# One-hot operands of the gate matmuls laid out contiguously in a three-layer mixer and expert kernel

## The reference, cut to what matters

```python
def peer(x, w_q, sub_keys, u_tab, v_tab):         # per token: 8 heads, 2 halves of 128 keys
    q = (xt @ w_q).reshape(T, PEER_HEADS, 2, PEER_HALF)
    s = jnp.einsum('thpd,hpkd->thpk', q, sub_keys)
    s_top, i_top = lax.top_k(s, PEER_TOPK)        # 16 best keys i1 and i2 of each half
    cand = s_top[:, :, 0, :, None] + s_top[:, :, 1, None, :]
    best, pos = lax.top_k(cand, PEER_TOPK)        # 16 pairs; expert = i1 * 128 + i2
    gate = jax.nn.softmax(best, axis=-1)
    act = gelu(einsum('td,thkd->thk', xt, u_tab[eid]))
    return einsum('thk,thkd->td', gate * act, v_tab[eid])
```

## Time and profile before

| | us |
|---|---|
| median of 3 runs | 3374.04 (3371.47 to 3375.68) |
| profiled execution, its time | 3377.82 |
| its span | 3376.0 |
| PE busy, PEld busy | 3158.0 (94%), 2855.7 (85%) |
| DVE busy | 2183.4 (65%) |
| ACT busy, POOL busy | 1602.8 (47%), 964.2 (29%) |

### The profile page before, as it was taken

The page is one execution under the profiler, slowest core; times in us unless marked ns, Lnnn a source line. Parts: engine busy times, 40 slices in busy tenths (PEclk is TensorE's granted clock), DMA queues, the critical chain, the costliest instruction groups (busy, mean ns, idle before and its releaser), DMA issues.

```text
span 3376.0 us, 65940 instructions
## 1 busy us (share of the span) xinstructions
PE 3158.0 (94%) x22842; PEld 2855.7 (85%) x22842; DVE 2183.4 (65%) x4301; ACT 1602.8 (47%) x2564; POOL 964.2 (29%) x377
## 2 busy tenths in 40 slices
PE   7899999999998879999999999778789999999998
PEld 6799999888787669999988878677689999988886
DVE  4387477777555345937777755686629667777755
ACT  3355433566455225543356645443345543366654
POOL 5578400000006437960000000256368920000000
PEclk9899999999999779999999999799899999999999
DMA  5445444444664224554444466333254544444554
GB/s 189 133 154 174 162 144 147 144 149 149 214 193 139 86 75 169 173 171 146 144 144 149 148 203 193 102 105 122 68 170 149 179 157 143 144 149 148 162 193 150
DMA packets 141398, 509.40 MB, mean 151 GB/s; under 512 B 16736, under 2 KB 17888, under 8 KB 140912
## 3 DMA queue, kind: packets, MB, share of 16 engines
q1 hardware_dynamic: 141296, 508.04, 45.9%
HBM read 506.93 MB, written 1.05 MB: 150 GB/s over the span
## 4 chain that ended last, share of the span: by engine, by line
PE 80%; DVE 8%; POOL 4%; issue 3%; ACT 2%; DMA 1%; SPq 0%; ACTq 0%; POOLq 0%; DVEq 0%
PE col L504 12%; PE col L506 12%; PE col L505 12%; PE acc L504 11%; PE acc L506 11%; PE acc L505 11%; POOL w_lo L461 4%; PE acc L631 4%; PE col L631 4%; ACT w_hi L719 1%; DVE work L1995 1%; PE acc L1498 1%; PE acc L600 1%; DMA ring<-in_ab_in 0%; DMA ring<-in_v 0%
## 5 line engine op out<-in xcount | busy, mean ns | idle before, releaser
L461 POOL TENSOR_TENSOR w_lo<-ring,w_hi 128x1024 fp32r<-128x1024 f32 x373 | 964.0, 2597 | 1765.7 <-ACT w_hi L719 1763.3
L719 ACT ACTIVATE w_hi<-ring 128x1024 fp32r<-128x1024 f32 x940 | 992.8, 1056 | 667.0 <-PE acc L506 529.5
L504 PE MATMUL col<-x_hi,w_hi 128*128 128x256 f32 (+1 forms) x3904 | 1125.0, 288 | 39.7 <-POOL w_lo L461 31.8
L505 PE MATMUL col<-x_lo,w_hi 128*128 128x256 f32 (+1 forms) x3904 | 1104.3, 283 | 0.0
L506 PE MATMUL col<-x_hi,w_lo 128*128 128x256 f32 (+1 forms) x3904 | 1103.9, 283 | 0.0
L461 DVE TENSOR_TENSOR w_lo<-ring,w_hi 128x1024 fp32r<-128x1024 f32 x567 | 692.6, 1222 | 229.4 <-ACT w_hi L719 229.3
L504 PEld LDWEIGHTS col<-x_hi,w_hi 128*128 128x128 f32 x3904 | 746.9, 191 | 48.6 <-issue 20.0
L506 PEld LDWEIGHTS col<-x_hi,w_lo 128*128 128x128 f32 x3904 | 744.3, 191 | 0.0
L505 PEld LDWEIGHTS col<-x_lo,w_hi 128*128 128x128 f32 x3904 | 741.6, 190 | 0.0
L504 PE MATMUL acc<-w_hi,c_hi 128*128 128x512 f32 x1664 | 670.0, 403 | 15.4 <-DVE c_lo L993 7.9
L506 PE MATMUL acc<-w_hi,c_lo 128*128 128x512 f32 x1664 | 651.6, 392 | 0.0
(11 more groups left out here) (289 smaller groups left out, 2516.7 us busy)
## 6 DMA issues: line engine op xcount, KB each, us to landing
ring<-in_u SPq DMA_DIRECT2D x384, 512.0 KB, 3.2
ring<-in_v SPq DMA_DIRECT2D x384, 512.0 KB, 3.6
ring<-in_wq SPq DMA_DIRECT2D x48, 512.0 KB, 3.2
ring<-in_s_in SPq DMA_DIRECT2D x32, 512.0 KB, 3.5
ring<-in_c_in SPq DMA_DIRECT2D x16, 512.0 KB, 3.2
ring<-in_c_wide SPq DMA_DIRECT2D x16, 512.0 KB, 3.2
ring<-in_s_out SPq DMA_DIRECT2D x16, 512.0 KB, 3.5
ring<-in_s_wide SPq DMA_DIRECT2D x12, 512.0 KB, 3.6
```

Of the source, the lines that this page charges most:

```text
L461: eng.tensor_tensor(k.w_lo[s.slot][:, :], k.ring[s.slot][:, :], k.w_hi[s.slot][:, :].bitcast(F32), ALU.subtract).then_inc(k.lo[s.slot], 1)
L504: pe.matmul(out, a[0], b[0], start=start, stop=False, **kw)
L505: pe.matmul(out, a[0], b[1], start=False, stop=False, **kw)
L719: act.activation(k.w_hi[s.slot][:, :], k.ring[s.slot][:, :], ACT.Copy).then_inc(k.hi[s.slot], 1)
```

## The change

The one-hots are stored with the key number i innermost, so that a token's 128 weights columns and its 64 moving columns are each one contiguous run. DVE still writes them with bf16 operands whose innermost step is one: i1, i2 and the gate parts are each stored twice in a row (`pairs`, `gate_all`), and the compare and multiply run over rows of two elements, with the number table `iota_b` read in pairs and repeated over the tokens. The four-fold table `iota_t` goes. The mask has one buffer instead of two, and `onehots` waits for the previous batch's `oh2` before it writes the mask. The buffers of the one-hots get shapes of their own, the gate's remainder is kept in `oh2`'s room, and the third mixer's scratch (`am`, `e`, `ones`) is mapped to the new buffers. ACT's late one-hots keep their operations and write contiguously.

```diff
-        self.oh1 = room[:, 0:GB * P].bitcast(BF16).rearrange("p (j i t) -> p j i t", j=2, t=GB)
+        self.oh1_all = sb("onehot_i1", [P, 2, GB, P], BF16)
+        self.oh1 = self.oh1_all[:, :, :, :]
+        self.pairs = sb("pairs_of_i1_i2", [P, 2, T, 2], BF16)
+        self.i1, self.i2 = self.pairs[:, 0, :, :], self.pairs[:, 1, :, :]
+        self.oh2_all = sb("gated_onehot_i2", [P, 2, PARTS, GB, EARLY], BF16)
+        self.mask2 = sb("mask_i2", [P, GB, EARLY], BF16)
+        self.gate_all = sb("pairs_of_gate", [P, BATCHES, PARTS, GB, 2], BF16)
+        self.rest = self.oh2.rearrange("p j n t i -> p (j n t i)")[:, 0:2 * T].bitcast(F32)
-        self.iota_t = sb("iota_by_token", [P, P, GB], BF16)
...
-                    ins = pe.matmul(banks[b.slot][:, t * EARLY:(t + 1) * EARLY], k.oh1[:, b.base % 2, :, t],
-                                    k.oh2[:, b.base % 2, n, :, t], start=n == 0, stop=n == PARTS - 1)
+                    ins = pe.matmul(banks[b.slot][:, t * EARLY:(t + 1) * EARLY], k.oh1[:, b.base % 2, t, :],
+                                    k.oh2[:, b.base % 2, n, t, :], start=n == 0, stop=n == PARTS - 1)
...
-                act.activation(k.oh1[:, 1, :, t], k.iota_b[:, :], ACT.Abs, bias=k.neg_i1[:, at])\
+                act.activation(k.oh1[:, 1, t, :], k.iota_b[:, :], ACT.Abs, bias=k.neg_i1[:, at])\
...
-        own.do(dve.tensor_scalar(k.i1[:, :], k.neg_i1[:, :], -1.0, None, ALU.mult))
-        own.do(dve.tensor_copy(k.i2[:, :], k.acc[0][:, T:2 * T]))
+        own.do(dve.tensor_scalar(k.i1, k.neg_i1[:, :].unsqueeze(2).to_broadcast([P, T, 2]), -1.0, None, ALU.mult))
+        own.do(dve.tensor_copy(k.i2, k.acc[0][:, T:2 * T].unsqueeze(2).to_broadcast([P, T, 2])))
...
-            own.do(dve.tensor_copy(k.gate[:, n, :], rest))
+            own.do(dve.tensor_copy(k.gate[:, :, n, :, :], rest.unsqueeze(3).to_broadcast([P, BATCHES, GB, 2])))
...
-            dve.tensor_tensor(k.mask2[:, slot, :, :], k.iota_t[:, at:at + EARLY, :],
-                              k.i2[:, tokens].unsqueeze(1).to_broadcast([P, EARLY, GB]), ALU.is_equal)\
+            if wait:
+                dve.wait_ge(k.oh_ready, b.index() + g0)
+            dve.tensor_tensor(mask, pairs[:, at // 2:(at + EARLY) // 2, :].unsqueeze(1).to_broadcast(shape),
+                              k.i2[:, tokens, :].unsqueeze(2).to_broadcast(shape), ALU.is_equal)\
                .then_inc(k.mask_ready, 1)
             if slot == 0 or not late:
-                dve.tensor_tensor(k.oh1[:, slot, :, :], k.iota_t[:, :, :],
-                                  k.i1[:, tokens].unsqueeze(1).to_broadcast([P, P, GB]), ALU.is_equal)
+                shape = [P, GB, P // 2, 2]
+                dve.tensor_tensor(k.oh1[:, slot, :, :].rearrange("p t (i two) -> p t i two", two=2),
+                                  pairs.unsqueeze(1).to_broadcast(shape),
+                                  k.i1[:, tokens, :].unsqueeze(2).to_broadcast(shape), ALU.is_equal)
             dve.wait_ge(k.mask_ready, b.index() + (g0 + 1))
-            shape = [P, PARTS, EARLY, GB]
-            dve.tensor_tensor(k.oh2[:, slot, :, :, :], k.mask2[:, slot, :, :].unsqueeze(1).to_broadcast(shape),
-                              k.gate[:, :, tokens].unsqueeze(2).to_broadcast(shape), ALU.mult)\
+            shape = [P, PARTS, GB, EARLY // 2, 2]
+            dve.tensor_tensor(k.oh2[:, slot, :, :, :].rearrange("p n t (i two) -> p n t i two", two=2),
+                              mask.unsqueeze(1).to_broadcast(shape),
+                              k.gate[:, bass.ds(b.index(), 1), :, :, :].rearrange("p b n t two -> p (b n) t two")
+                              .unsqueeze(3).to_broadcast(shape), ALU.mult)\
                .then_inc(k.oh_ready, 1)
```

More of the change, by code:

```diff
@@ L1072, in peer @@
         w.next(k.i1_ready)
-        own.do(dve.tensor_scalar(k.i1[:, :], k.neg_i1[:, :], -1.0, None, ALU.mult))
-        own.do(dve.tensor_copy(k.i2[:, :], k.acc[0][:, T:2 * T]))
-        rest = k.acc[0][:, 0:T]
+        own.do(dve.tensor_scalar(k.i1, k.neg_i1[:, :].unsqueeze(2).to_broadcast([P, T, 2]), -1.0, None, ALU.mult))
+        own.do(dve.tensor_copy(k.i2, k.acc[0][:, T:2 * T].unsqueeze(2).to_broadcast([P, T, 2])))
+        rest = k.acc[0][:, 0:T].rearrange("p (b t) -> p b t", t=GB)
+        left = k.rest.rearrange("p (b t) -> p b t", t=GB)
         for n in range(PARTS):
-            own.do(dve.tensor_copy(k.gate[:, n, :], rest))
+            own.do(dve.tensor_copy(k.gate[:, :, n, :, :], rest.unsqueeze(3).to_broadcast([P, BATCHES, GB, 2])))
             own.join()
             if n + 1 < PARTS:
-                own.do(dve.tensor_tensor(k.rest, rest, k.gate[:, n, :], ALU.subtract))
+                own.do(dve.tensor_tensor(left, rest, k.gate[:, :, n, :, 0], ALU.subtract))
                 own.join()
-                rest = k.rest
+                rest = left
         experts = view(k.big, 0, KEYS, T)
@@ L1090, in onehots @@
             _, at, g0 = k.gate_pass(layer, late)
-            if wait:
+            if b.turn is not None or b.base + g0 > 1:
                 dve.wait_ge(k.g_full, b.index() + (g0 - 1))
             slot, tokens = b.base % 2, bass.ds(b.index() * GB, GB)
-            dve.tensor_tensor(k.mask2[:, slot, :, :], k.iota_t[:, at:at + EARLY, :],
-                              k.i2[:, tokens].unsqueeze(1).to_broadcast([P, EARLY, GB]), ALU.is_equal)\
+            pairs = k.iota_b[:, :].rearrange("p (i two) -> p i two", two=2)
+            shape = [P, GB, EARLY // 2, 2]
+            mask = k.mask2[:, :, :].rearrange("p t (i two) -> p t i two", two=2)
+            if wait:
+                dve.wait_ge(k.oh_ready, b.index() + g0)
+            dve.tensor_tensor(mask, pairs[:, at // 2:(at + EARLY) // 2, :].unsqueeze(1).to_broadcast(shape),
+                              k.i2[:, tokens, :].unsqueeze(2).to_broadcast(shape), ALU.is_equal)\
                .then_inc(k.mask_ready, 1)
             if slot == 0 or not late:
-                dve.tensor_tensor(k.oh1[:, slot, :, :], k.iota_t[:, :, :],
-                                  k.i1[:, tokens].unsqueeze(1).to_broadcast([P, P, GB]), ALU.is_equal)
+                shape = [P, GB, P // 2, 2]
+                dve.tensor_tensor(k.oh1[:, slot, :, :].rearrange("p t (i two) -> p t i two", two=2),
+                                  pairs.unsqueeze(1).to_broadcast(shape),
+                                  k.i1[:, tokens, :].unsqueeze(2).to_broadcast(shape), ALU.is_equal)
             dve.wait_ge(k.mask_ready, b.index() + (g0 + 1))
-            shape = [P, PARTS, EARLY, GB]
-            dve.tensor_tensor(k.oh2[:, slot, :, :, :], k.mask2[:, slot, :, :].unsqueeze(1).to_broadcast(shape),
-                              k.gate[:, :, tokens].unsqueeze(2).to_broadcast(shape), ALU.mult)\
+            shape = [P, PARTS, GB, EARLY // 2, 2]
[3 more added lines that the diff above has]
+                              .unsqueeze(3).to_broadcast(shape), ALU.mult)\
                .then_inc(k.oh_ready, 1)
@@ L1123, in peer @@
         for n in range(2):
-            onehots(Slab(n), 0, wait=k.gates_before(layer, 0) > 0)
+            onehots(Slab(n), 0, wait=k.gates_before(layer, 0) + n > 0)
         dve.wait_ge(k.evac, k.cols_before[k.first[f"u{layer}"] + EARLY])
@@ L1182, in vector_program @@
     dve.wait_ge(k.const, 32)
-    e.own.do(dve.tensor_copy(k.iota_b[:, :], k.iota[:, :]))
-    e.own.do(dve.tensor_copy(k.iota_t[:, :, :], k.iota[:, :].unsqueeze(2).to_broadcast([P, P, GB])))
+    e.own.do(dve.tensor_copy(k.iota_b[:, :], view(k.big, JUNK, P)))
+    e.own.do(dve.tensor_copy(k.iota[:, :], view(k.big, JUNK, TOPK)))
     dve.wait_ge(k.xload, 16 * NT)
@@ L1725, in __init__ @@
                                   for part in (k.c_hi, k.c_lo))
-        self.am = [k.oh1_room[:, j, 0:self.UNIT, :] for j in range(2)]
-        self.e = [k.oh2_room[:, j, 0:self.UNIT, :] for j in range(2)]
-        self.ones = k.oh1_room[:, 0, 3, :]
+        rooms = [room.rearrange(f"p {names} -> p ({names})").bitcast(F32)
+                 for room, names in ((k.oh2, "j n t i"), (k.gate, "b n t two"))]
+        self.e, self.am = ([room[:, j * self.UNIT * P:(j + 1) * self.UNIT * P].rearrange("p (r l) -> p r l", l=P)
+                            for j in range(2)] for room in rooms)
+        self.ones = k.oh1.rearrange("p j t i -> p (j t i)").bitcast(F32)[:, 0:P]
         self.yT = self.xdecay.rearrange("p t c -> p (t c)").rearrange("p (n t) -> p n t", t=T)
```

18 lines of the change are left out of this document (4 added, 14 removed).

## The result

The kernel after takes **3236.7 us** (median of 4 runs, 3234.68 to 3240.04), the kernel before beside it 3374.86 us (4 runs, 3371.47 to 3375.85). The ratio is 0.9594 with a 95% interval of 0.9579 to 0.9609. The forecast was 3273 us, within 3235 to 3380; the result lies inside, but only 2 us above the lower end. The profiled execution took 3240.04 us, 137.8 less than that of before (3377.8).

A forecast was written before the change was run, and what follows sets the result against it. TensorE was taken to bound the kernel, each nanosecond off a gate matmul's pitch coming off the end. The profiled 3377.8 - 104 (gate matmuls) + 3 (heads) = 3276.8 us, median 3.8 below: 3273 us, range 3235 to 3380.

The forecast's parts named there:

- That strided reading holds the 62 ns: TensorE's gate matmuls: reading operands 8 bytes from element to element from SBUF was held likeliest to set the 62 ns pitch.
- The rival of no gain: Gate matmuls: 62 ns is a fixed cost of a bf16 load and matmul pair, not layout; 3377 us, chance 0.23.
- the 62 ns of sequencer work: Trainium skill's bound per matmul in one decoding mode, about 62 ns, cited as speaking against a gain.
- the partial rival: Gate matmuls: only one operand was slow, the other holds the pitch at 55 ns; 3347 us, chance 0.13.
- the prediction's reader: SBUF operand reader with its own clock, getting one strided element where it gets two adjacent: 53 ns and some overhead.
- The 70 ns at half clock: Average pitch of four gate matmuls near 384 us at 1.2 GHz, read as the limit hardly knowing the array's clock.
- the 27 ns of the earlier trace: Pitch of contiguous load and matmul pairs (16 weight, 24 moving columns), used against an issue limit and as lower bound.
- The size of the gain per batch: Twelve gate matmuls: pitch from 62 to 38 ns, 0.27 us off each of 384 batches, 104 us in all.
- The first matmul behind the batch: Slab's first matmul after the gate batch: its weights wait a little; 0.01 us off, bounds 0 and 0.08.
- VectorE's step: Mask, `oh1`, `oh2`: rows of two taken as packed, cost 0, 285, 434 and 560 ns; unpacked 421, 690 and 955.
- The late 0.29: VectorE's wait before `weigh` in the late pass: falls from 0.56 to 0.29 us a step, so VectorE remains covered.
- The head: Start of the early pass, three times: mask and `oh1` can fall behind POOL's last split; + 1.0 us a layer, 3 in all.

The follow-up runs named there:

- the run with 64: Kernel after, each gate matmul split into two of 32 columns, with 64 instead of 128 weight columns: 3475.34 us, ratio 1.0306 to the kernel before.

## Why the prediction was right

**That strided reading holds the 62 ns** was argued by exclusion and is now shown: the same instructions at 8 bytes apart take 3373.75 us, at 2 bytes 3236.7. The rival of no gain falls, and with it the 62 ns of sequencer work: the same instructions run at 29. So does the partial rival: with both operands contiguous neither holds the pitch near 53 ns. The picture of the reader was right in that its pace doesn't follow TensorE's clock (60 ns at either), and wrong in its unit. It wasn't "one strided element where it gets two adjacent ones" but one 16-byte line for 1.8 to 1.9 ns: by the prediction's reader 4, 8 and 16 bytes apart would have cost the same, and they cost 31, 60 and 116 ns.

The two rules of the Trainium skill that spoke against it fare so. Its page "SBUF — State Buffer" (the note on cachelines in the section on Door 1) names lines of 16 bytes, and the runs at 16 and 32 bytes agree; but it asks for two hits a line, and two hits (8 bytes apart) cost 60 ns instead of 29. With 1.8 to 1.9 ns a line from the table, and 0.42 ns a column at 2.4 GHz (106.7 / 256), the array takes four columns in 1.7 ns, so four hits are about what keeps up, and four (4 bytes apart) gave 29 to 33 ns. At 1.2 GHz two hits nearly do: 32 lines are 60 ns beside 53 for the columns. The page "TensorE: Matmul & The Clock Gate" (Weight-path perf modes) names packed and strided weights side by side for the fast load, without a price; here strided ones cost 33 against 29 ns, and 118 against 98 for the load. The same section switches the fast load on only for 128 weights, and the run with 64 agrees.

Two readings on the way there were weaker than they looked. The 70 ns at half clock stand for three single pitches of 89, 53 and 62 ns: the first pitch of a batch is longer (57 ns at full clock), and only the other two bear on the question. And the 27 ns of the earlier trace rows were read at half clock too, which the prediction doesn't say:

```profile
2178.60:2179.10 0.50, 0.50 (x23) 0.50 (x22) 0.00 (x0) 0.00 (x0) 0.00 (x0) 0.50 0.00 0
```

**The size of the gain per batch** is the term that was off: 0.27 us forecast, 0.36 measured, 104 against 138 us. The step that failed is "a gate matmul with 64 columns would by the same count cost 26.7 + 11 = 38 ns". The 10 to 11 ns beside a slab matmul's columns were taken for a fixed overhead of any matmul. They aren't: a contiguous gate matmul takes 29 to 30 ns, 26.7 of columns and 3 beside them. In the slab itself they come and go with the clock: in the kernel after, in a stretch of half clock, slab matmuls follow each other at (2640.65 - 2640.01) / 3 = 213 ns, 256 columns at 1.2 GHz with nothing added.

```profile
2640.00:2642.00 2.00, 2.00 (x12) 2.00 (x11) 2.00 (x4) 0.00 (x0) 0.00 (x0) 0.50 0.10 41
```

```profile
2640.01 0.41 PE L500 MATMUL col<-x_hi,w_hi 128*128 128x256 f32 x1
...
2640.65 0.41 PE L500 MATMUL col<-x_hi,w_hi 128*128 128x256 f32 x1
```

What the slab's 117 ns at full clock are made of stays open; there are two rivals. By the line rule 256 fp32 columns are 64 lines, and 64 lines of bf16 took 116 to 118 ns. But then the 512-wide matmuls of the `v` slabs, with 128 lines, should take 232 to 236 ns, and they follow each other at (696.17 - 695.04) / 5 = 226. The other rival is the load of 128 fp32 weight columns, which the gate matmuls don't have. In the kernel before it shows with 24 moving columns, which would be 10 ns by their columns and 11 by their 6 lines, first at full clock (1.00 from 2171.00 to 2172.30 us), then at half (0.50 from 2175.70 to 2178.50 us):

```profile
2171.16 0.26 PE L504 MATMUL misc<-c_hi,x_hi 128*128 128x24 f32 x1
...
2172.05 0.26 PE L506 MATMUL misc<-c_hi,x_lo 128*128 128x24 f32 x1
```

```profile
2175.96 0.37 PE L504 MATMUL misc<-c_hi,x_hi 128*128 128x24 f32 x1
...
2176.81 0.37 PE L505 MATMUL misc<-c_lo,x_hi 128*128 128x24 f32 x1
```

That is 0.89 / 8 = 111 ns and 0.85 / 4 = 213 ns, so the load alone comes near the slab's 117 and 213. But it doesn't explain 226 ns for 512 columns, which are 213 ns. I changed nothing on the slab matmuls, so neither is shown.

For a 64-column gate pair, the 26.7 ns of columns lie just above the 25 ns that a pair with 32 columns takes; where the last 2 to 3 ns come from is open. The lower bound of 27 ns would have been the nearer value, 152 us less for the whole, 14 too much, but by luck: those pairs have fp32 weights and ran at half clock, where the same matmul with 128 instead of 16 weight columns takes 213 ns, eight times as long. So the 27 ns go with the 16 fp32 weight columns; the pair's fixed cost is at most that.

**The first matmul behind the batch**: 0.01 us forecast. It starts 29 instead of 47 ns behind the last gate matmul (single records), 0.018 us.

**VectorE's step** came as forecast: rows of two pack (301, 419 and 554 ns), and without pairs 428, 690 and 952 where 421, 690 and 955 were named. The mask takes 301 ns instead of the forecast 285. The early cover fell to 0.72 us, forecast 0.81, which is the forecast corrected for the larger gain. The late 0.29 was forecast for the wait before `weigh` alone, and that wait fell further, to 21.1 / 192 = 0.11 us a step; with the wait for `c_hi` the late cover is 0.33. ScalarE's wait "moves closer", as was said: 42.2 us against 25.1 before (line 993 then). That ScalarE's one-hots would get 169 ns shorter each was not foreseen. TensorE's idle time behind `c_lo` didn't grow, 7.7 us against 7.9.

**The head** had the right mechanism and too large a price: + 0.2 us a layer instead of + 1.0. The step said that the mask and `oh1` "can fall behind POOL's last split, and 0.29 + 0.42 us is then added". The mask did fall behind it, and now waits the split out in place of a later instruction. What is added is only what moves from before the split's end to behind it. In the second and third layer of the kernel before that later instruction was `oh1` (2.60 us, at 1496.13), and the gate matmul started 0.81 us behind the split's end (single records); now it is 1.01 us in every layer. In the first layer, the one of the earlier trace rows, it was `oh2`, 0.48 us behind the end, but there the split also ended 0.32 us later after the first copy's start than it does now.

**The sum** made again with the measured terms: 3377.8 - 138.2 + 0.6 = 3240.2, and the profiled execution took 3240.04. The sum that was forecast was 36 us too high, and by far the most of that is the gate pitch. Had only the weights been laid out anew, it would have been 3361, and with only the moving columns 3266.
